# A two-block hybrid layer on one core: all four routing chunks of token tiles 1 to 3 placed beside the preceding tile's experts

## Chip, cores and metric

One core of a Trainium2 chip runs the whole program. The metric is device time in microseconds (us) from one launch, as a median over runs.

## What is computed

Everything is fp32, batch 1, 256 tokens, model width 1024. A first block (gated recurrent branch, delta-rule branch, feed-forward) is followed by two hybrid layers. Each hybrid layer mixes four kinds of attention and then applies a product-key expert layer, which is the part at issue:

```python
def block(xi):                                   # 128 tokens
    qv = (xi @ wq).reshape(B, 128, 8, 2, 128)    # 8 heads, two halves
    s = jnp.einsum('bthpc,hpnc->bthpn', qv, sub_keys)
    top_s, top_i = lax.top_k(s, 16)              # 16 best of 128 keys per half
    cand_s = top_s[..., 0, :, None] + top_s[..., 1, None, :]
    best_s, best_j = lax.top_k(cand_s..., 16)    # 16 best of 256 pairs
    expert = take(cand_i, best_j); gate = softmax(best_s)
    act = gelu(einsum('btd,bthkd->bthk', xi, u_tab[expert]))
    return einsum('bthk,bthkd->btd', gate * act, v_tab[expert])
```

So each token picks 8 x 16 = 128 of 16384 experts, and each expert is one row of 1024 numbers in `u_tab` and one in `v_tab`. In the kernel the two tables lie side by side in one tensor `puv` with rows of 2048 numbers (8 KB).

## The kernel before, in words

**Tiles.** The 256 tokens are two tiles of 128, and there are two hybrid layers, so the second half of the program works through four token tiles, numbered 0 to 3 (tiles 0 and 1 are layer 0, tiles 2 and 3 layer 1). Tile i+2 needs the result of tile i, and some state goes from tile i to tile i+1, but the mixing part of tile i+1 does not need the experts of tile i. The kernel therefore runs the mixing part of tile i+1 beside the experts of tile i.

**Experts.** Expert step n = 128 i + k serves the k-th chosen expert of all 128 tokens of tile i. `fetch` on POOL (L2274) gathers 128 rows of `puv` (1 MB) into one of six buffers `GR` (`PING` = 6), after expert n-6 has left its buffer. `expert_ve` on DVE (L2290) multiplies the u half by the tokens and sums. `expert_ac` on ACT (L2259, L2261, L2264) applies gelu and the gate and scales the v half. `expert_pe` on PE (L2246) adds the eight transposed 128x128 pieces into PSUM banks 6 and 7.

**Query and route.** Per tile these come in four chunks c of two heads. `query_pe` (L2121) multiplies by the weights `pwq` in 8 steps, two loads of 1 MB, and `query_ac` (L2132) copies the result out. `route_pe` (L2142) does the key scores, `route_ac` (L2153) copies them to `S1`, and `route_ve` takes the two rounds of top 16 on DVE in steps (first instruction L2164, last before the indices are ready L2223) and writes the indices `IX` and gates. A chunk is 8 query and 20 route steps. Chunk c gives the experts 32c to 32c+31 of its tile: `fetch` waits for `TV[i, c, "ix"]` at those numbers.

**The plan.** The list `plan` (from L259) sets one order for all engines: each engine plays the steps of the plan in this order, and those in which it has nothing to do cost it nothing. An engine executes in order, so an instruction that waits holds back everything behind it there. Beside the 128 experts of tile i there is a main lane, the end of tile i-1 (`fin`, 8 of its steps) and all of `tile_steps(i + 1)`, spread by `weight` over 118 experts; `tile_steps` gives `fm` and `tm` (projections), `gates`, `nsa` and `core` woven together (attention), `mix` (output projection and norm), and `query` and `route` of chunk 0. A second lane holds chunks 1 to 3 of tile i itself, spread over its own first 33 experts. Tile 0 has no preceding tile and its first part runs ahead of all experts.

**Loads.** SP issues the weight loads of the four tiles (`loads2`, L2496) into a ring of five slots of 1 MB (`RING2`), in the order of first use in the plan. A load is issued when the load five before it has been used up. Queries of a tile read eight `pwq` loads, and the other parts of a tile about forty loads. The scratch that tile 0's own query and route chunks use (`QP`, `S1` and so on, from `scr`) is also that of the next tile's attention, so these must not overlap in the plan.

Of the kernel before, what the change touches and what calls it, by code (L numbers as in the profile page):

```python
# [40 lines left out]
def weave(parts, filler=None):  # L41


    left = {name: steps for name, steps, _ in parts}
    owed = dict.fromkeys([name for name, _, _ in parts] + ([filler[0]] if filler else []), 0.0)
    order = []
    while any(left.values()):
        for name, _, rate in parts:
            if left[name]:
                owed[name] += rate  # L50
                while owed[name] >= 1 and left[name]:
                    owed[name] -= 1
                    left[name] -= 1
                    order.append(name)
        if filler:
            owed[filler[0]] += filler[1]
            while owed[filler[0]] >= 1:
                owed[filler[0]] -= 1
                order.append(filler[0])
    return order  # L60
# [18 lines left out]
def build(nc, A, out):  # L79
# [4 lines left out]
    with ctx:  # L84
# [159 lines left out]
        R2, R3, R4, R6, R8 = range(2), range(3), range(4), range(6), range(8)  # L244
# [12 lines left out]
        NE = 512  # L257
        weight = dict(fm=1.06, ht1=1.5, tm=1.7, gates=1.7, nsa=1.2, core=1.5, mix=1.5, query=1.06, route=0.7, fin=1.0)

        def tile_steps(i):  # L260
            front = ["fm"] * 28 + ["ht1"] * (i == 0) + ["tm"] * 4 + weave([("tm", 10, 1), ("core", 7, 0.7)])
            attend = weave([("gates", 32, 1), ("nsa", 23, 1), ("core", 14, 0.7)])
            return front + attend + ["mix"] * 24 + ["query"] * 8 + ["route"] * 20

        plan = [(s, 0) for s in tile_steps(0)[:-36]]
        plan += [(s, 0) for s in tile_steps(0)[-36:]]
        for i in RI:
            placed_at = [(128.0 * i + k, ("e", 128 * i + k)) for k in range(128)]
            placed_at += [(128.0 * i + 1.1 + 0.1 * k, ("fin", i - 1)) for k in range(4) if i >= 1]
            lane = [("fin", i - 1)] * 8 * (i >= 1) + [(s, i + 1) for s in (tile_steps(i + 1) if i < 3 else [])]  # L270
            total, done = sum(weight[s] for s, _ in lane), 0.0
            for s in lane:
                placed_at.append((128.0 * i + 1.5 + 118 * done / total if i < 3 else 128.0 * i + 1.5 + done, s))
                done += weight[s[0]]
            lane = []
            for c in R3:
                lane += [("query", i)] * 8 + [("route", i)] * 20
            for n, s in enumerate(lane):
                placed_at.append((128.0 * i + 0.2 + 33.0 * n / len(lane), s))
            plan += [s for _, s in sorted(placed_at, key=lambda x: x[0])]  # L280
        plan += [("e", NE), ("e", NE + 1)] + [("fin", 3)] * 12

# [5 lines left out]
                    nsa=[("cw", 0, 0, 2)], gates=[("g", n, 2 * n, 4 * (n // 2) + 3) for n in range(16)],  # L288
                    mix=[("b", n, 2 * n + 2, 2 * n + 3) for n in R4] + [("o", n, 12 + n, 12 + (n | 1)) for n in R4] + [("ga", 0, 19, 21)],
                    query=[("q", n, 4 * n, 8 * (n // 2) + 7) for n in R8], fin=[("gf", 0, 8, 9)])  # L290
        step, nth2, last2 = {}, {}, {}
        for at_, s in enumerate(plan):
            n = step[s] = step.get(s, -1) + 1
# [2351 lines left out]
```

## Time and profile before

| what | value |
|---|---|
| runs (device time) | 2823.6, 2828.5 and 2821.54 us, median 2823.6 |
| profiled execution, span from first to last instruction | 2818.2 us |
| PE busy in it | 2309.7 us (82%) |
| DVE busy | 1353.8 us (48%) |
| ACT busy | 1299.6 us (46%) |
| POOL busy | 742.4 us (26%) |
| DMA moved | 839.32 MB, mean 298 GB/s |
| first to last expert fetch | 1098.5 to 2790.9 us |

The profile covers one execution. Its page gives the span of instructions only, without a time of its own for what lies around it: the span is 5.4 us under the median of the three runs. Busy shares are over the whole span, in which two very different halves lie: up to 1098.5 us the first block and tile 0's mixing part, then the 512 experts.

### The profile page before, as it was taken

The page shows a single profiled execution, that of the slowest core. Times are in us where ns is not written, and L with a number is a line of the kernel's source. Part 1 is how long each engine was busy: PE and PEld are TensorE (multiplying, and loading weights), DVE is VectorE, ACT ScalarE, POOL GpSimd, SP SyncE. Part 2 cuts the span into 40 slices and gives each one's busy share as a digit, 9 for nine tenths or more (in the row PEclk, how much of TensorE's full clock was granted, in tenths as well). Part 3 has the DMA queues.
Part 4 walks back from the last instruction along what each step waited for, and adds up shares of the span by engine and source line. Part 5 has one row for each costly group of instructions (what it writes and reads, how often), then busy time and mean ns, then how long its engine had stood idle before and what let it go on. Part 6 is the DMA issues. An engine that isn't in the chain of part 4 may idle for free.

```text
span 2818.2 us, 33729 instructions
## 1 busy us (share of the span) xinstructions
PE 2309.7 (82%) x13336; PEld 1955.2 (69%) x13336; DVE 1353.8 (48%) x3183; ACT 1299.6 (46%) x2327; POOL 742.4 (26%) x614
## 2 busy tenths in 40 slices
PE   7989998999999995887876877787788787666666
PEld 6878887876875875776755866666777675565554
DVE  3552333321002234666456765545766545686444
ACT  2751113100000212577745576844658764566665
POOL 0021112200000001233333323333323333334554
PEclk9989999999999997999996999898799899776665
DMA  5321211133434666999999999999999999999997
GB/s 241 117 90 60 78 65 45 53 138 144 151 150 156 253 236 258 421 408 416 399 421 403 411 421 419 408 421 421 390 420 410 414 383 420 393 365 363 417 421 311
DMA packets 109998, 839.32 MB, mean 298 GB/s; under 512 B 12176, under 2 KB 12432, under 8 KB 13968
## 3 DMA queue, kind: packets, MB, share of 16 engines
q0 software_dynamic: 73728, 536.90, 46.6%
q1 hardware_dynamic: 36112, 300.25, 27.0%
q8 instruction: 106, 1.74, 0.2%
q14 instruction: 52, 0.43, 0.0%
HBM read 836.06 MB, written 1.05 MB: 297 GB/s over the span
## 4 chain that ended last, share of the span: by engine, by line
PE 48%; DMA 24%; DVE 12%; ACT 10%; issue 4%; POOL 2%; SPq 0%; POOLq 0%; DVEq 0%; ACTq 0%
DMA mem<-in_puv,mem 23%; PE psm L442 11%; PE psm L2246 6%; PE psm L450 5%; DVE mem L2290 4%; PE psm L755 4%; PE psm L1809 4%; ACT mem L2264 3%; PE psm L2121 3%; PE psm L1350 3%; PE psm L1453 2%; PE psm L2008 2%; ACT L2259 1%; PE psm L1501 1%; PE psm L446 1%
## 5 line engine op out<-in xcount | busy, mean ns | idle before, releaser
L2246 PE MATMUL psm<-mem 128*128 128x128 f32 x4096 | 682.1, 322 | 363.6 <-ACT mem L2264 361.2
L2274 POOL DMA_INDIRECT mem<-in_puv,mem x512 | 621.1, 1213 | 1059.9 <-PE psm L2246 993.3
L2246 PEld LDWEIGHTS psm<-mem 128*128 128x128 f32 x4096 | 566.5, 167 | 475.7 <-ACT mem L2264 459.8
L2290 DVE CUSTOM_DVE_ANT_0 mem<-mem 128x1024 f32<-128x1024 f32 x512 | 624.5, 1225 | 471.3 <-DMA mem<-in_puv,mem 470.8
L2264 ACT ACTIVATE mem<-mem 128x1024 f32<-128x1024 f32 x512 | 588.8, 1150 | 16.7
L442 PE MATMUL psm<-mem 128*128 128x256 f32 (+2 forms) x1376 | 313.0, 390 | 3.1 <-DVE mem L1290 1.5
L2259 ACT ACTIVATE mem<-mem 128x1 f32<-128x1 f32 x512 | 101.9, 199 | 437.7 <-DVE mem L2290 434.5
L442 PEld LDWEIGHTS psm<-mem 128*128 128x128 f32 x1376 | 261.8, 192 | 53.2 <-issue 14.8
L1809 PE MATMUL psm<-mem 128*128 128x256 f32 x1024 | 256.0, 398 | 0.5 <-ACT mem L1529 0.5
L450 PEld LDWEIGHTS psm<-mem 128*128 128x128 f32 x1440 | 187.2, 196 | 49.1 <-issue 21.4
L450 PE MATMUL psm<-mem 128*128 128x128 f32 x1440 | 199.3, 283 | 22.6 <-DVE mem L1125 6.8
L1809 PEld LDWEIGHTS psm<-mem 128*128 128x128 f32 x1024 | 197.3, 202 | 26.9 <-ACT mem L1529 0.9
L2261 ACT ACTIVATE mem<-mem 128x1 f32<-128x1 f32 x512 | 150.8, 295 | 16.6
L755 PE MATMUL psm<-mem 128*128 128x256 f32 x576 | 151.6, 387 | 0.0
L2121 PE MATMUL psm<-mem 128*128 128x128 f32 x1024 | 139.3, 293 | 2.3 <-DMA mem<-in_pwq 1.0
L2121 PEld LDWEIGHTS psm<-mem 128*128 128x128 f32 x1024 | 133.6, 210 | 4.5 <-DVE mem L2104 2.0
L1035 ACT ACTIVATE mem<-psm 128x512 f32<-128x512 f32 x64 | 38.2, 597 | 201.5 <-PE psm L450 134.6
L1453 PE MATMUL psm<-mem 128*128 128x128 f32 x896 | 113.5, 280 | 6.9 <-DVE mem L2334 3.8
L1453 PEld LDWEIGHTS psm<-mem 128*128 128x128 f32 x896 | 108.0, 197 | 8.2 <-DVE mem L2334 4.5
L755 PEld LDWEIGHTS psm<-mem 128*128 128x128 f32 x576 | 100.7, 195 | 7.9
L446 PE MATMUL psm<-mem 128*128 128x128 f32 (+1 forms) x352 | 60.6, 310 | 54.0 <-DVE mem L484 13.3
L446 PEld LDWEIGHTS psm<-mem 128*128 128x128 f32 (+1 forms) x352 | 45.8, 158 | 68.4 <-issue 26.2
(364 smaller groups left out, 2365.7 us busy)
## 6 DMA issues: line engine op xcount, KB each, us to landing
mem<-in_w2g SPq DMA_DIRECT2D x64, 1024.0 KB
mem<-in_w SPq DMA_DIRECT2D x18, 2048.0 KB, 8.2
mem<-in_pwq SPq DMA_DIRECT2D x32, 1024.0 KB
mem<-in_w2f SPq DMA_DIRECT2D x28, 1024.0 KB
mem<-in_wgu SPq DMA_DIRECT2D x11, 2048.0 KB, 7.7
mem<-in_w2t SPq DMA_DIRECT2D x20, 1024.0 KB
mem<-in_w2b SPq DMA_DIRECT2D x16, 1024.0 KB
mem<-in_w2o SPq DMA_DIRECT2D x16, 1024.0 KB
```

The lines of the kernel that those rows point to most:

```text
L442: m = pe.matmul(o, lhs(k), rhs(k), start=start and k == ks[0], stop=stop and k == ks[-1])
L446: return pe.transpose(o, i, ident[0:i.shape[0], 0:i.shape[0]])
L450: m = pe.matmul(b[:, u * 128:u * 128 + 128], lhs(u), rhs(u), start=True, stop=True)
L755: m = pe.matmul(o, W[:, k, c0:c0 + 128], HT[:, k, :], start=k == 0, stop=k == 7)
L1453: m = pe.matmul(o, W[:, k, h * 128:h * 128 + 128], HT[:, k, tsl(t)], start=k == 0, stop=k == 7)
L1809: m = pe.matmul(gates_bank(i, n // 2)[:, n % 2 * 256:n % 2 * 256 + 256], HT[:, k, tsl(t)], W[:, k, :], start=k == 0, stop=k == 7)
L2121: m = pe.matmul(o, W[:, k, h * 128:h * 128 + 128], HT[:, k, tsl(t)], start=k == 0, stop=k == 7)
L2246: m = pe.matmul(bank(6 + c // 4)[:, tsl(c % 4)], GR[n % PING][:, 1024 + c * 128:1152 + c * 128], ident, is_transpose=True, start=k == 0 an ...
L2261: ac.activation(co, co, ACT.Copy, scale=g).then_inc(oa.up(), 1)
L2264: ac.activation(v, v, ACT.Copy, scale=co).then_inc(EA.next(n), 1)
L2274: po.indirect_dma_start(GR[n % PING], None, A[f"puv{i // 2}"], bass.IndirectOffsetOnAxis(ap=IX[i % 2][:, k:k + 1], axis=0)).then_inc(gsem[ ...
L2290: ve.tensor_tensor_reduce(out=GR[n % PING][:, 0:1024], in0=GR[n % PING][:, 0:1024], in1=X[:, i % 2, :], scale=1.0, scalar=0.0, op0=MUL, op ...
```

## The change

`EARLY = (1, 2, 3)` names tiles whose four query and route chunks are all part of `tile_steps`, and so of the main lane beside the preceding tile's experts. The second lane is empty for these, and for tile 0 it holds chunks 1 to 3 over 28 experts in place of 33. For tile 1, 16 of the 32 `gates` steps go ahead of the woven attention, which keeps tile 1's attention behind tile 0's own chunks. No instruction is added or removed; line numbers of the changed kernel are 4 higher from the plan on.

```diff
--- before.py
+++ after.py
@@ -257,10 +257,13 @@
         NE = 512
         weight = dict(fm=1.06, ht1=1.5, tm=1.7, gates=1.7, nsa=1.2, core=1.5, mix=1.5, query=1.06, route=0.7, fin=1.0)
 
+        EARLY = (1, 2, 3)
+
         def tile_steps(i):
             front = ["fm"] * 28 + ["ht1"] * (i == 0) + ["tm"] * 4 + weave([("tm", 10, 1), ("core", 7, 0.7)])
-            attend = weave([("gates", 32, 1), ("nsa", 23, 1), ("core", 14, 0.7)])
-            return front + attend + ["mix"] * 24 + ["query"] * 8 + ["route"] * 20
+            ahead = 16 * (i in EARLY and i - 1 not in EARLY)
+            attend = ["gates"] * ahead + weave([("gates", 32 - ahead, 1), ("nsa", 23, 1), ("core", 14, 0.7)])
+            return front + attend + ["mix"] * 24 + (["query"] * 8 + ["route"] * 20) * (4 if i in EARLY else 1)
 
         plan = [(s, 0) for s in tile_steps(0)[:-36]]
         plan += [(s, 0) for s in tile_steps(0)[-36:]]
@@ -273,10 +276,11 @@
                 placed_at.append((128.0 * i + 1.5 + 118 * done / total if i < 3 else 128.0 * i + 1.5 + done, s))
                 done += weight[s[0]]
             lane = []
-            for c in R3:
-                lane += [("query", i)] * 8 + [("route", i)] * 20
+            lane = []
+            if i not in EARLY:
+                lane = ([("query", i)] * 8 + [("route", i)] * 20) * 3
             for n, s in enumerate(lane):
-                placed_at.append((128.0 * i + 0.2 + 33.0 * n / len(lane), s))
+                placed_at.append((128.0 * i + 0.2 + 28.0 * n / len(lane), s))
             plan += [s for _, s in sorted(placed_at, key=lambda x: x[0])]
         plan += [("e", NE), ("e", NE + 1)] + [("fin", 3)] * 12
```

Two places show what moves. PE, one whole chunk, from the key scores of one chunk (L2142, or L2146 in the changed kernel) to those of the next; L2121 (L2125) are query matmuls and L2246 (L2250) the eight transposes of each expert. Before, this is from tile 3's chunk 1 to its chunk 2, beside tile 3's own experts:

```order
L2142 MATMUL psm<-mem 128x128 x4
L2246 MATMUL psm<-mem 128x128 x64
L2121 MATMUL psm<-mem 128x128 x12
L2246 MATMUL psm<-mem 128x128 x8
L2121 MATMUL psm<-mem 128x128 x8
L2246 MATMUL psm<-mem 128x128 x8
L2121 MATMUL psm<-mem 128x128 x12
L2246 MATMUL psm<-mem 128x128 x8
L2142 MATMUL psm<-mem 128x128 x4
```

With the change, from tile 3's chunk 0 to its chunk 1, beside tile 2's experts:

```order
L2146 MATMUL psm<-mem 128x128 x4
L2250 MATMUL psm<-mem 128x128 x48
L2125 MATMUL psm<-mem 128x128 x12
L2250 MATMUL psm<-mem 128x128 x8
L2125 MATMUL psm<-mem 128x128 x8
L2250 MATMUL psm<-mem 128x128 x8
L2125 MATMUL psm<-mem 128x128 x12
L2250 MATMUL psm<-mem 128x128 x8
L2146 MATMUL psm<-mem 128x128 x4
```

Before, 64 transposes (8 experts) follow the key scores and 3 more lie among the query matmuls, 11 experts per chunk; now 6 and 3, 9 experts (in the order of the changed kernel a chunk in the main lane has 8 or 9, and over the nine distances between the four chunks of tiles 1 to 3 the mean is 8.8). The same 32 query matmuls and 4 score matmuls stand among fewer experts.

SP, the last loads of the program, from the output projection's weights of tile 3 (`in_w2b`, `in_w2o`; `in_rows` are norm weights). Before:

```order
L2496 DMA mem<-in_w2b 128x2048 x4
L2496 DMA mem<-in_w2o 128x2048 x4
L2496 DMA mem<-in_rows 128x2048
L2496 DMA mem<-in_pwq 128x2048 x4
L2496 DMA mem<-in_rows 128x2048
L2496 DMA mem<-in_pwq 128x2048 x4
L2496 DMA mem<-in_rows 128x2048
L2507 DMA out<-mem 128x1024 x2
```

and with the change:

```order
L2500 DMA mem<-in_w2b 128x2048 x4
L2500 DMA mem<-in_w2o 128x2048 x4
L2500 DMA mem<-in_rows 128x2048
L2500 DMA mem<-in_pwq 128x2048 x8
L2500 DMA mem<-in_rows 128x2048 x2
L2511 DMA out<-mem 128x1024 x2
```

The last `in_rows` before the output belongs to tile 3's final norm, the one before it to tile 2's. Six of tile 3's eight query loads stood around tile 2's norm weights, where tile 3's own experts run; now all eight are ahead of it.

## Rows read from the trace of the kernel before

**Rows 1.** the page, busy time and the 40 slices of 70.5 us
```profile
PE 2309.7 (82%) x13336; PEld 1955.2 (69%) x13336; DVE 1353.8 (48%) x3183; ACT 1299.6 (46%) x2327; POOL 742.4 (26%) x614
...
PEclk9989999999999997999996999898799899776665
DMA  5321211133434666999999999999999999999997
GB/s 241 117 90 60 78 65 45 53 138 144 151 150 156 253 236 258 421 408 416 399 421 403 411 421 419 408 421 421 390 420 410 414 383 420 393 365 363 417 421 311
```

**Rows 2.** stretches with busy time of each engine, the last tile without and with routing
```profile
core 0: us, PE busy (x) PEld busy (x) DVE busy (x) ACT busy (x) POOL busy (x), PEclk, DMA share, GB/s
2577.00:2777.00 200.00, 137.54 (x635) 110.08 (x634) 98.39 (x160) 130.17 (x238) 117.86 (x80) 0.64 1.01 420
2500.00:2580.00 80.00, 54.89 (x341) 48.48 (x340) 57.80 (x180) 50.51 (x90) 31.73 (x28) 0.72 0.89 328
```

**Rows 3.** waits from 1130 us on: who for whom, us in total, times, longest
```profile
POOL mem L2274 <- PE psm L2246: 976.2, 436, 8.1
DVE mem L2290 <- DMA mem<-in_puv,mem: 461.3, 294, 5.0
```

**Rows 4.** the same view, own chunks 1 to 3 of tiles 1 and 2
```profile
1560.00:1680.00 120.00, 98.06 (x752) 91.72 (x751) 86.10 (x275) 73.81 (x128) 36.38 (x33) 0.96 1.01 414
2015.00:2130.00 115.00, 98.16 (x718) 91.03 (x716) 83.72 (x269) 73.19 (x125) 34.89 (x31) 0.91 1.01 417
```

**Rows 5.** DVE in order of time, last two own chunks of tile 3: start, us, line
```profile
2508.14 0.88 DVE L2164 MAX8 mem<-mem 128x8 f32<-128x128 f32 x4 [7.00 <-ACT mem L2153]
...
2530.06 0.19 DVE L2223 SCALAR_TENSOR_TENSOR mem<-mem 128x32 uint32<-128x32 f32 x1
...
2543.06 0.68 DVE L2164 MAX8 mem<-mem 128x8 f32<-128x128 f32 x3 [7.22 <-ACT mem L2153]
...
2564.99 0.19 DVE L2223 SCALAR_TENSOR_TENSOR mem<-mem 128x32 uint32<-128x32 f32 x1
```

**Rows 6.** stretches, the last own chunk whole, then its two halves
```profile
2530.10:2565.10 35.00, 25.10 (x161) 22.23 (x160) 27.17 (x90) 21.55 (x38) 12.55 (x11) 0.74 0.89 330
2530.10:2543.10 13.00, 12.56 (x102) 12.32 (x102) 5.41 (x16) 8.92 (x17) 4.25 (x4) 0.90 0.81 307
2543.10:2565.10 22.00, 12.54 (x62) 9.91 (x60) 21.76 (x75) 12.63 (x22) 8.30 (x7) 0.65 0.94 344
```

**Rows 7.** by line: DVE over 2495 to 2565 us, PE over 2530.1 to 2565.1 us
```profile
L2290 DVE CUSTOM_DVE_ANT_0 mem<-mem 128x1024 f32<-128x1024 f32 x22 | 26.4, 1216 | 0.9 <-DMA mem<-in_puv,mem 0.9
...
L2246 PE MATMUL psm<-mem 128*128 128x128 f32 x89 | 16.7, 345 | 9.9 <-ACT mem L2264 9.9
L2121 PE MATMUL psm<-mem 128*128 128x128 f32 x64 | 8.8, 301 | 0.0
```

**Rows 8.** stretches, tile 3's chunk 0 and the 10 us behind it
```profile
2385.00:2431.00 46.00, 26.82 (x187) 23.23 (x185) 31.38 (x88) 22.96 (x41) 15.77 (x15) 0.83 1.01 421
2430.00:2440.00 10.00, 5.32 (x25) 5.29 (x26) 7.64 (x17) 8.28 (x17) 3.15 (x3) 0.50 0.75 288
```

**Rows 9.** DVE in order of time, chunk 0 of tile 3: first and last step
```profile
2407.84 0.88 DVE L2164 MAX8 mem<-mem 128x8 f32<-128x128 f32 x4
...
2431.04 0.19 DVE L2223 SCALAR_TENSOR_TENSOR mem<-mem 128x32 uint32<-128x32 f32 x1
```

**Rows 10.** stretches, gates and attention of tiles 1, 2 and 3
```profile
1231.00:1418.00 187.00, 150.38 (x968) 129.62 (x967) 103.73 (x225) 132.54 (x235) 71.49 (x59) 0.93 1.00 409
1679.00:1870.00 191.00, 148.95 (x917) 127.70 (x916) 97.83 (x224) 137.94 (x245) 67.20 (x59) 0.91 1.01 415
2125.00:2322.00 197.00, 160.52 (x1010) 139.13 (x1007) 105.69 (x229) 139.86 (x243) 70.30 (x62) 0.92 0.99 401
```

**Rows 11.** stretch of tile 1's second and third own chunk, first experts of tile 0
```profile
1141.00:1231.00 90.00, 72.68 (x497) 65.78 (x496) 59.06 (x190) 59.10 (x101) 23.28 (x22) 0.91 1.01 414
```

**Rows 12.** the page, DMA issues by source
```profile
mem<-in_pwq SPq DMA_DIRECT2D x32, 1024.0 KB
```

## The prediction

> **What bounds the kernel now.** I read the page first [rows 1]. PE is busy 82% of the span, which looks like the bound, but the DMA line says otherwise for the second half: from slice 17 on, where the expert fetches begin, it shows 9 in all but one slice, at 399 to 421 GB/s in most. The best view of what this means is the last tile, where only experts are left [rows 2]: 200 us at DMA share 1.01 and 420 GB/s, with PE, DVE and ACT at half to two thirds. The waits agree [rows 3]: DVE's expert step waited 461 us for the gathers. So in the second half the kernel moves a fixed number of bytes at up to 421 GB/s, and a stretch costs time only where the rate is lower. One load or one expert fetch is 1.049 MB, which is 2.49 us at 421 GB/s; I count in these.
>
> Where is the rate lower? Mainly in the last tile, between 2500 and 2580 us [rows 2]: 328 GB/s over 80 us, a loss of 80 x (1 - 328/421) = **17.7 us**. There tile 3's own chunks 2 and 3 stand beside its own experts and no other tile's work exists. The same kind of chunk beside tiles 1 and 2 [rows 4] runs at 414 and 417 GB/s, since `fm` and `tm` of the next tile bring loads of their own to fill the rate. So a routing chunk is harmless beside a stage with many loads, and costs time without one.
>
> **How long one chunk takes when loads don't cover it.** The two index writes (L2223) of tile 3's last chunks are at 2530.1 and 2565.0 us [rows 5], 35 us apart with 11 experts between. In these 35 us DVE is busy 27.2 us [rows 6]: 11 experts at 1.22 us plus the read-out, some 1.30 us each, so 14.3, and 12.9 us for the chunk's top-16 work. It falls into two halves. In the first, 13 us, DVE mostly waits, 7.2 us in one piece, for the copy of the scores (L2153) [rows 5], while PE is busy 12.6 of 13 us with query matmuls and backed-up transposes [rows 6]. In the second, 22 us, DVE is busy 21.8. The queries alone are 8.8 us of PE per chunk [rows 7]. PE cannot start the next chunk's queries early: in its order they stand behind transposes of experts that DVE has not reached. So PE's half and DVE's half follow one another, whatever DMA could do.
>
> **The change, part by part.**
>
> *Tile 3's own chunks go.* Its experts then run like the 200 us of [rows 2] from the end of tile 2's norm on. Gain: the 17.7 us. The fewer query loads there (six of 1 MB) are no gain, they move to the stage before. **-17.7 us.**
>
> *Four chunks in a row beside the preceding tile's experts.* Chunk 0 stands there already: 46 us at 421 GB/s, then 10 us at 288 [rows 8]. It is covered by what is in flight, up to six fetches and the ring's five loads, and the drop behind it shows that the cover is then used up. I take chunk 0 as unchanged. Behind it now come three more per tile, nine in all, and what is beside them is only 8.8 experts and two query loads each [rows 12]: 10.8 MB, or 26.9 us of transfer. How long does each take? From the 35.0 us, 2.2 experts of 1.30 us fewer on DVE, 32.1 us, if the 7.9 us in which DVE idles stay. Low bound: part of the idle goes as well, as fewer transposes lie before the queries (2.2 experts at PE's 16.7/11 = 1.5 us [rows 7], 3.3 us): 28.8. High bound: chunk 0's DVE half took 23.2 us with only six experts [rows 9]; with the 13 us of the other half, 36.2. The nearest row is the tail's own cycle, so I stay by 32.1 and add half a microsecond because chunk 0's DVE half was the longer one: 32.6 us. Loss per chunk 32.6 - 26.9 = 5.7, nine times: **+51 us** (bounds 9 x 1.9 = 17 and 9 x 9.3 = 84). SP's queue is no extra wait here: the query loads follow each other in the ring as before. The cover is not renewed between chunks, as a ring slot frees only with the queries and a buffer only with its expert.
>
> A page states a higher ceiling: the Trainium skill, "Perfetto Trace Analysis", section Roofline, takes about 120% of 358 GB/s, thus 430, as what a single core can reach. By that figure as an estimate the transfers of a chunk would be 26.4 us and the loss nearly 5 us larger over nine chunks; the trace holds 420 to 421 [rows 2, 8] and I stay with it.
>
> *The own lane of tiles 1 and 2 is empty.* That stage was at 414 and 417 GB/s [rows 4], bound by bytes, and stays so with fewer. Gain at most 120 x (1 - 414/421) = 2 us; the wait of `fin` stays. **0.** If DMA did not cover it, 0 would be wrong, but it is what ends last there.
>
> *The other stages get fewer experts.* The main lane now holds more, over the same 118 experts, so gates and attention have about 41 experts where 57 ran in the 187 to 197 us of [rows 10]. Bytes per step fall, PE's work per step doesn't. Before: PE busy 149 of 191 us in tile 2's stretch. Less 16 experts at 1.2 us (1.5 at granted clock 0.74 [rows 6, 7], here 0.91), 130; the transfers are 41 + 17 loads, 144 us. So PE goes from 78% to 90%, still under the bytes, yet with less room. The three stretches already lose 5, 3 and 9 us against 421 GB/s. Between no more loss and twice this, 0 to +17, I take **+8**.
>
> *Tile 0's own chunks in 28 experts for 33, tile 1's gates ahead.* Before, 414 GB/s with PE busy 73 of 90 us [rows 11]. 16 gates steps cost PE and DMA about the same as the mix there; bounds 0 and +5, taken as 0, with bytes from tile 1's `fm`, `tm` and gates as the cover.
>
> Sum: -17.7 + 51 + 8 = **+41 us**. The profiled span of 2818.2 would become 2859; its distance of 5.4 us to the median lies in what surrounds the span and in scatter, so on the median of 2823.6 I forecast **2865 us**. Bounds: -17.7 + 17 = -1 and -17.7 + 84 + 17 + 5 = +88.
>
> **Rivals.**
>
> *A, faster: the bytes cover the chunks.* If the four chunks together with what is in flight never let the rate fall below 421, only the 17.7 us of tile 3 are left: 2806 us. The place is chunks 1 to 3 beside the preceding tile; it decides at 26.9 + 17.7/9 = 28.9 us per chunk, under which the whole is a gain. The Trainium skill, "Perfetto Trace Analysis", section Identifying the Most-Contended Engine, says to go by the engine with the highest occupancy; by that, DMA is the one here and moving DVE's work within a stage that DMA bounds is free. For it: chunk 0 ran at 421 GB/s [rows 8], and the own lanes too [rows 4]. Against it: the tail's 35 us cycles with PE and DVE taking turns [rows 6], and the 10 us at 288 right after a single chunk. 10%.
>
> *B, no change: cover for about half.* The chunks overlap better than in the tail, 29 to 30 us each, and tile 3's gain pays. Sum within 8.5 us of zero: 2824 us. For it: the granted clock is 0.65 in the DVE half and 0.90 in the other [rows 6], and where it stays up PE's half is shorter. Against: the same alternation. 8%.
>
> *C, slower still: PE becomes the bound of gates and attention.* If PE's idle there is dependency and not slack, the 16 experts fewer save little time, 10 us per tile instead of 3: three times 10, plus 51 less 17.7, gives 2887 us or more. For it: in the stretch of tile 3 PE was busy 160.5 of 197 us and the rate only 401 [rows 10]. 10%.
>
> That the change does not do what it says is not open: the order of both engines shows it.
>
> **How the numbers follow.** A measurement of this kernel tells a difference of about 0.3%, 8.5 us, from none. The forecast (cycle 31 to 35 us, 2835 to 2885 us) has 72%, A 10%, B 8%, C 10%. The forecast and C are slower by over 0.3%, 0.82; B is the same, 0.08; A is faster, 0.10. For 8 in 10 the range leaves out A, part of B and part of C: 2828 to 2895 us.
>
> **What would show it.** In the changed profile: three times per expert tile, a stretch of some 100 us before the next tile begins with 340 to 360 GB/s, each chunk 31 to 35 us from one index write to the next, DVE's wait for the score copy some 7 us each time, and the DMA line of the page at 8 there; the last tile at 420 GB/s from its first experts on, its fetches over in about 325 to 330 us. Index writes 27 us apart and 421 GB/s throughout would prove me wrong and A right; gates and attention under 390 GB/s would be C.

## The result, and the profile after

The changed kernel takes 2923.2 us (median of 4 runs, 2919.9 to 2929.7), the kernel before 2822.6 us in the same comparison: ratio 1.0365, 95% interval 1.0343 to 1.0387. I had forecast a loss of 41 us, 2865 us with a range of 2828 to 2895; it is 100 us. The direction was right, the size lies outside the range.

The page of the changed kernel, busy time and the 40 slices (now of 73 us), against [rows 1]:

```profile
PE 2351.5 (81%) x13336; PEld 1992.3 (68%) x13336; DVE 1354.7 (46%) x3183; ACT 1304.8 (45%) x2331; POOL 748.5 (26%) x614
...
PEclk9989999999999998898977888987699998766666
DMA  6221111234435569899998999998899999799997
GB/s 245 106 95 71 62 51 44 80 130 149 168 136 225 219 228 374 355 402 376 369 365 328 389 404 417 405 421 331 346 404 385 379 412 394 294 358 421 421 421 322
```

PE, DVE and ACT are busy for the same time within 2%; the same work is done. One thing was said wrongly ahead of the result: instructions are added, four on ACT (x2331 against x2327), all of them `ACT_TABLE_LOAD` of 1.28 us, 5.1 us together. They are not what makes the difference, as e2 and e10 below have 2327 and still lose 45 and 54 us. The DMA line, 9 nearly throughout before, now dips to 8 or 7 in every tile but the last, and the rates fall to 294 and 328 GB/s in places. The four chunks of tiles 1, 2 and 3, without their chunk 0, and a stretch of the last tile (columns as in [rows 2]):

```profile
1487.00:1592.00 105.00, 65.15 (x426) 59.30 (x425) 75.74 (x252) 54.78 (x96) 30.48 (x28) 0.78 0.88 341
1969.00:2071.00 102.00, 62.59 (x419) 57.15 (x418) 75.01 (x251) 53.01 (x94) 31.24 (x27) 0.75 0.88 343
2455.00:2558.00 103.00, 64.46 (x418) 58.95 (x417) 74.09 (x249) 52.99 (x93) 30.86 (x26) 0.75 0.81 303
2600.00:2800.00 200.00, 138.35 (x635) 110.81 (x636) 98.71 (x160) 130.88 (x238) 121.48 (x80) 0.64 1.01 421
```

The first three are the regions that I had described: 341, 343 and 303 GB/s with DVE busy for about three quarters of them. The last tile runs as foretold, 421 GB/s. DVE in order of time in the last region shows the cycles and the waits, against [rows 5] (L2227 is the index write, L2168 the first top-16 step):

```profile
2455.07 0.18 DVE L2227 SCALAR_TENSOR_TENSOR mem<-mem 128x32 uint32<-128x32 f32 x1
...
2487.93 0.18 DVE L2227 SCALAR_TENSOR_TENSOR mem<-mem 128x32 uint32<-128x32 f32 x1
...
2502.36 0.49 DVE L2168 MAX8 mem<-mem 128x8 f32<-128x128 f32 x2 [8.33 <-ACT mem L2157]
...
2521.37 0.19 DVE L2227 SCALAR_TENSOR_TENSOR mem<-mem 128x32 uint32<-128x32 f32 x1
...
2539.37 0.49 DVE L2168 MAX8 mem<-mem 128x8 f32<-128x128 f32 x2 [11.46 <-ACT mem L2157]
...
2558.35 0.19 DVE L2227 SCALAR_TENSOR_TENSOR mem<-mem 128x32 uint32<-128x32 f32 x1
```

Index writes are 32.9, 33.4 and 37.0 us apart here, over all nine chunks 31.9 to 37.0, mean 34.3. Where four experts stand between an index write and the next scores, DVE's wait for these is 7.0 to 8.3 us and the cycle 32.8 us in the mean (four cycles); where five do, the wait is 9.3 to 11.5 us but for one of 6.3, and the cycle 35.6 us (five cycles).

**Where the 100 us went.** I cut both traces at DVE's marks (index writes, first step of the mix, norm, first step of the final part `fin`) and took for each piece its length times (1 - rate/421), as in the prediction. The sums are worked out from the stretches view, from 1100 us to tile 3's final norm, and are in us of lost transfer:

| stage | before | after | difference |
|---|---|---|---|
| tile 0's own chunks 1 to 3 | 2.8 | 13.3 | +10.5 |
| projections, attention and mix of tile 1 | 5.3 | 20.9 | +15.6 |
| the same of tile 2, with what own lane there is beside it | 4.6 | 11.8 | +7.2 |
| the same of tile 3 | 11.9 | 21.1 | +9.2 |
| chunk 0 of tiles 1 to 3 | 0.0 | 0.0 | 0 |
| the nine chunks that were moved, beside the preceding tile | none | 67.4 | +67.4 |
| from the last chunk to `fin`, three times | 9.0 | 19.5 | +10.5 |
| last tile from `fin` on | 28.0 | 8.2 | -19.8 |
| sum | 61.6 | 162.2 | +100.6 |

The spans differ by 100.0 us. That the two agree proves nothing by itself: both kernels move the same 839.32 MB, so whatever time is lost must show as a lower rate somewhere. The table says which stages lose it, not why. Two thirds are the nine chunks; the 20 us won in the last tile are there as well; and 43 us are in stages for which I had set 8.

The stages ahead of the routing in the changed kernel: end of tile 0's own lane, attention of tile 1, and the whole of tile 2's and tile 3's projections and attention, against [rows 10, 11]:

```profile
1178.00:1233.00 55.00, 37.59 (x207) 33.17 (x208) 31.47 (x106) 35.62 (x58) 9.32 (x9) 0.81 0.87 338
1233.00:1400.00 167.00, 140.79 (x823) 121.63 (x822) 83.13 (x187) 111.39 (x189) 48.50 (x44) 0.87 0.93 376
1618.00:1875.00 257.00, 210.21 (x1344) 184.35 (x1344) 120.62 (x267) 169.95 (x301) 78.29 (x74) 0.89 0.99 402
2097.00:2360.00 263.00, 216.95 (x1424) 192.31 (x1425) 129.65 (x273) 173.25 (x303) 80.76 (x73) 0.92 0.96 387
```

PE is busy 68%, 84%, 82% and 82% of these: below the 90% that I had feared for attention, and yet bytes are lost, which a bound by an engine's busy time does not explain.

### The profile page after: what moved, and what is told of

Its sections match the earlier page's. It is cut to its first block, busy times and chain, and to the rows that moved or that the text cites. A ratio compares the mean times of both kernels' runs of the same rounds, so it can differ in the third digit from the quotient of the medians.

```text
span 2918.2 us, 33733 instructions
## 1 busy us (share of the span) xinstructions
PE 2351.5 (81%) x13336; PEld 1992.3 (68%) x13336; DVE 1354.7 (46%) x3183; ACT 1304.8 (45%) x2331; POOL 748.5 (26%) x614
## 2 busy tenths in 40 slices
DMA packets 109998, 839.32 MB, mean 288 GB/s; under 512 B 12176, under 2 KB 12432, under 8 KB 13968
## 4 chain that ended last, share of the span: by engine, by line
PE 52%; DMA 17%; DVE 14%; ACT 10%; issue 4%; POOL 2%; SPq 0%; POOLq 0%; DVEq 0%; ACTq 0%
DMA mem<-in_puv,mem 16%; PE psm L446 11%; PE psm L2250 7%; PE psm L454 5%; PE psm L1813 5%; DVE mem L2294 4%; PE psm L759 4%; PE psm L1457 3%; ACT mem L2268 3%; PE psm L2125 3%; PE psm L1354 3%; PE psm L2012 2%; PE psm L1505 2%; ACT L2263 2%; PE psm L450 1%
## 5 line engine op out<-in xcount | busy, mean ns | idle before, releaser
L2250 PE MATMUL psm<-mem 128*128 128x128 f32 x4096 | 703.5, 329 | 416.1 <-ACT mem L2268 413.3
L2250 PEld LDWEIGHTS psm<-mem 128*128 128x128 f32 x4096 | 583.8, 171 | 529.5 <-ACT mem L2268 509.4
L446 PEld LDWEIGHTS psm<-mem 128*128 128x128 f32 x1376 | 262.7, 193 | 52.8 <-issue 14.8
L454 PEld LDWEIGHTS psm<-mem 128*128 128x128 f32 x1440 | 187.5, 196 | 49.1 <-issue 21.5
L454 PE MATMUL psm<-mem 128*128 128x128 f32 x1440 | 199.6, 284 | 22.7 <-DVE mem L1129 6.8
L1813 PEld LDWEIGHTS psm<-mem 128*128 128x128 f32 x1024 | 194.6, 198 | 26.6 <-issue 1.2
L2125 PE MATMUL psm<-mem 128*128 128x128 f32 x1024 | 145.8, 303 | 4.4 <-DVE mem L2108 3.2
L2125 PEld LDWEIGHTS psm<-mem 128*128 128x128 f32 x1024 | 140.9, 220 | 6.0 <-DVE mem L2108 4.7
L1457 PE MATMUL psm<-mem 128*128 128x128 f32 x896 | 109.3, 278 | 0.7 <-ACT mem L1372 0.7
L759 PEld LDWEIGHTS psm<-mem 128*128 128x128 f32 x576 | 101.1, 196 | 8.0
L1457 PEld LDWEIGHTS psm<-mem 128*128 128x128 f32 x896 | 105.6, 195 | 0.9 <-DVE mem L1377 0.9
## 6 DMA issues: line engine op xcount, KB each, us to landing
mem<-in_w2t SPq DMA_DIRECT2D x20, 1024.0 KB, 11.9
```

Source lines behind the costliest of these rows:

```text
L446: m = pe.matmul(o, lhs(k), rhs(k), start=start and k == ks[0], stop=stop and k == ks[-1])
L454: m = pe.matmul(b[:, u * 128:u * 128 + 128], lhs(u), rhs(u), start=True, stop=True)
L759: m = pe.matmul(o, W[:, k, c0:c0 + 128], HT[:, k, :], start=k == 0, stop=k == 7)
L1457: m = pe.matmul(o, W[:, k, h * 128:h * 128 + 128], HT[:, k, tsl(t)], start=k == 0, stop=k == 7)
L1813: m = pe.matmul(gates_bank(i, n // 2)[:, n % 2 * 256:n % 2 * 256 + 256], HT[:, k, tsl(t)], W[:, k, :], start=k == 0, stop=k == 7)
L2125: m = pe.matmul(o, W[:, k, h * 128:h * 128 + 128], HT[:, k, tsl(t)], start=k == 0, stop=k == 7)
```

## The experiments

In most runs theory A is the prediction's mechanism: a chunk's query half on PE and its route half on DVE follow one another, and 8.8 experts and two loads don't fill that time. Theory B, in its forms, puts the loss elsewhere. All ratios are to the kernel before, run beside it; the changed kernel stands at 1.0365.

**e1: queries of the next chunk among this chunk's route steps.**

```diff
+        def chunks_(n):
+            out = ["query"] * 8
+            for _ in range(n - 1):
+                out += (["route"] * 2 + ["query"]) * 8 + ["route"] * 4
+            return out + ["route"] * 20
-            return front + attend + ["mix"] * 24 + (["query"] * 8 + ["route"] * 20) * (4 if i in EARLY else 1)
+            return front + attend + ["mix"] * 24 + chunks_(4 if i in EARLY else 1)
```

> The changed kernel with the eight query steps of chunk c+1 played among the first sixteen route steps of chunk c for tiles 1 to 3, and nothing else. Theory A (the loss is PE's query half and DVE's route half of a chunk following one another): the halves overlap, the index writes come closer to 27 or 28 us apart instead of 34, and of the 75 us that the rate loses in these regions some 50 come back: 2860 to 2880 us. Theory B (the loss comes from the other stages having fewer experts beside them, and the regions only show it): 2915 to 2930 us, no change.

2865.3 us, ratio 1.0158 (1.0131 to 1.0184): 58 us came back, as theory A said. The same three regions in its trace:

```profile
1494.00:1572.00 78.00, 48.08 (x336) 44.44 (x336) 71.69 (x244) 49.92 (x86) 27.81 (x24) 0.83 1.01 421
1957.00:2035.00 78.00, 46.40 (x320) 41.81 (x320) 69.88 (x241) 48.23 (x83) 27.27 (x23) 0.86 1.01 414
2427.00:2504.00 77.00, 47.70 (x330) 42.58 (x328) 69.67 (x240) 48.23 (x83) 25.56 (x24) 0.82 0.95 375
```

421, 414 and 375 GB/s where it was 341, 343 and 303, in 78 us where it was 102 to 105. DVE is busy about 90% of it. Its wait for the scores, from DVE's order of time:

```profile
2458.18 0.49 DVE L2174 MAX8 mem<-mem 128x8 f32<-128x128 f32 x2 [1.75 <-ACT mem L2163]
...
2485.24 0.29 DVE L2174 MAX8 mem<-mem 128x8 f32<-128x128 f32 x1 [1.75 <-ACT mem L2163]
```

is 1.75 us here, and 0.9 to 1.9 in the eight chunks that wait, in place of 6 to 11. Lost in the nine chunks: 10 us, from 67. The same steps and loads stand there in another order, beside 70 experts where it was 79, and yet less is lost: the alternation is shown to be the cause of this part. The attention stages lose about what they lost (15.6, 13.5 and 22.3 us, where it was 18.3, 11.8 and 21.0).

**e2: only tile 3 early** (`EARLY = (3,)`; all own lanes 28 experts, tile 3's gates ahead).

> EARLY = (3,): only tile 3's four chunks stand beside tile 2's experts; tiles 1 and 2 keep their own lane, as short as tile 0's in the changed kernel, 28 experts, and tile 3 has the 16 gates steps ahead. Theory A: one region of three extra chunks, 25 to 32 us lost, 20 us gained in the last tile, little else: 2825 to 2840 us. Theory B: the single dense lane costs 10 to 20 us more than that and the gates steps ahead 10 more: 2845 to 2860 us.

2867.7 us, ratio 1.0175 (1.0141 to 1.0208), above what either theory gave. It mixes several edits; e3 to e5 take them apart in part.

**e3: own lanes shortened from 33 to 28 experts in the kernel before.**

```diff
-                placed_at.append((128.0 * i + 0.2 + 33.0 * n / len(lane), s))
+                placed_at.append((128.0 * i + 0.2 + 28.0 * n / len(lane), s))
```

> The kernel before with 28.0 for 33.0 in the own lane of every tile and nothing else. Theory A: these chunks have cover by the next tile's loads, so no change, 2820 to 2828 us. Theory B: the start of each tile gets too dense for PE and in-order waits, 4 us and more per tile: 2835 us and more.

2858.0 us, ratio 1.0138 (1.0108 to 1.0168): 35 us for five experts' room, theory B's side and far more than I thought. In tile 3, which has no loads to cover them, the three chunks run at

```profile
2480.00:2586.00 106.00, 67.11 (x416) 59.98 (x414) 78.87 (x251) 52.46 (x92) 29.91 (x28) 0.73 0.83 304
```

304 GB/s with 29.6 us lost in the three pieces between index writes, 17 before. The rest is spread over the stages ahead of the routing, 6 to 8 us more in each of the three tiles. Only the spacing of the routing steps was changed: the closer they stand, the fewer bytes are beside them.

**e4: 16 of tile 1's gates steps ahead of its attention, in the kernel before.**

```diff
-            attend = weave([("gates", 32, 1), ("nsa", 23, 1), ("core", 14, 0.7)])
+            ahead = 16 * (i == 1)
+            attend = ["gates"] * ahead + weave([("gates", 32 - ahead, 1), ("nsa", 23, 1), ("core", 14, 0.7)])
```

> The kernel before with 16 of tile 1's 32 gates steps ahead of its woven attention, and nothing else. Theory A: no change within 5 us, since bytes bind. Theory B: the attention that is left has fewer loads and matmuls beside it and ends in a stretch with no load at all, 10 to 17 us as between 1370 and 1400 us of the changed kernel's trace: 2833 to 2840 us.

2836.7 us (seven runs, 2826.7 to 2840.7), ratio 1.0041 (1.0023 to 1.0060), some 12 us slower, 7 to 17 by the interval: theory B. The stretches view shows it at the end of tile 1's attention, where the gates steps and their loads have run out:

```profile
1410.00:1450.00 40.00, 30.26 (x150) 25.74 (x150) 22.86 (x49) 28.91 (x51) 9.78 (x10) 0.67 0.72 263
1239.00:1447.00 208.00, 162.39 (x970) 141.11 (x970) 104.11 (x226) 135.17 (x236) 69.66 (x59) 0.86 0.95 384
```

263 GB/s for 40 us, in which no load is issued; the whole attention stage loses 18.3 us where it lost 5.3 (the trace is of the slowest of the seven runs, so rather the high end). This is a part of the change that I had set at nothing.

**e5: one region, nothing else that can be avoided** (the changed kernel with `EARLY = (3,)`, `ahead = 0`, own lanes `33.0 if i < 2 else 28.0`), and **e6: the same with e1's weaving.**

> EARLY = (3,), no gates steps ahead, own lanes of tiles 0 and 1 over 33 experts as before and tile 2's over 28: one region of three extra chunks, with as little else changed as the scratch allows. Theory A (the region itself loses): 25 to 32 us lost in it, 20 us won in the last tile, 5 us for the denser lane beside it: 2833 to 2842 us. Theory B (what e2 lost is in the short own lanes and the gates, the region is free): 2803 to 2815 us.

> The kernel of e5 with the query steps of chunk c+1 among the route steps of chunk c in that region. Theory A: of the 25 to 32 us of the region about 20 come back, so 2815 to 2824 us, about 20 us under e5. Theory B: like e5.

2842.0 us, ratio 1.0075 (1.0049 to 1.0100), and 2824.0 us, ratio 1.0012 (0.9994 to 1.0031). The region of three chunks, e5 and then e6:

```profile
2377.00:2480.00 103.00, 64.14 (x419) 58.64 (x417) 74.14 (x249) 52.99 (x93) 30.53 (x27) 0.75 0.81 307
```

```profile
2387.00:2465.00 78.00, 48.20 (x321) 43.12 (x320) 70.19 (x242) 48.30 (x83) 27.20 (x23) 0.82 0.95 376
```

27.9 us lost in e5's and 8.3 in e6's, and the runs differ by 18. Both came out as theory A said, e5 at the upper end of its range, e6 at the top of its own: one tile moved costs 20 us, weaving gives nearly all of it back, and then the move is worth nothing. The stage of tile 3 ahead of the region loses 19 us in e5 and 29 in e2, which has 16 of tile 3's gates steps ahead of its attention: e4's effect at another tile.

**e7: only tile 3's own chunks woven, in the kernel before.**

```diff
+            if i < 3:
+                lane = ([("query", i)] * 8 + [("route", i)] * 20) * 3
+            else:
+                lane = [(s, i) for s in chunks_(3)]
```

> The kernel before, with only tile 3's own chunks 1 to 3 woven (queries of the next chunk among the route steps of this one), all else the same. Theory A: the alternation is what holds the rate at 328 GB/s from 2500 to 2580 us, so 10 to 15 us of the 17.7 are won: 2807 to 2813 us. Theory B (DVE's own work is the bound there, or the wait for the gathers): no change, 2820 to 2825 us.

2810.9 us, ratio 0.9966 (0.9950 to 0.9983), within theory A's range and, by the medians, 11 us faster than the kernel before. The 328 GB/s of [rows 2] became

```profile
2500.00:2560.00 60.00, 38.09 (x240) 33.13 (x240) 53.71 (x178) 42.09 (x73) 23.07 (x20) 0.77 1.00 392
```

**e8: the changed kernel with tile 0's own lane over 33 experts again** (`28.0` to `33.0`).

> The changed kernel with tile 0's own lane over 33 experts again in place of 28. If the short lane costs here what it costs in e3 at the start of tile 0 (some 8 us between 1190 and 1240 us): 2912 to 2917 us. If it is nothing without the other lanes: 2920 to 2926 us.

2928.4 us, ratio 1.0392 (1.0357 to 1.0426): above both expectations, and its interval overlaps that of the changed kernel (1.0343 to 1.0387), so slower is not shown; its fastest run, 2927.5 us, is 10 us above what a gain by the longer lane would have given. With the gates steps ahead, tile 0's last chunk then stands among more of tile 1's steps: the third chunk lost 17.0 us there, 10.8 in the changed kernel, and the attention behind it 15.1, where it was 18.3. The short lane is no loss in this place.

**e9: tile 1's remaining gates steps spread over its whole attention** (rate 0.7 in the weave).

> The changed kernel with tile 1's 16 remaining gates steps spread over its whole attention (rate 0.7 in the weave, where it was 1), so that loads and matmuls do not end seven iterations before the attention does. Theory A (the 17 us lost between 1370 and 1410 us come from a stretch with dependent small steps and no loads): 10 us come back, 2910 to 2916 us. Theory B (the attention is slow there whatever stands beside it): 2920 to 2926 us.

2922.1 us, ratio 1.0361 (1.0344 to 1.0378), no change, as theory B said. Tile 1's attention and mix lost 14.7 us in place of 20.9, but its chunks lost 2.9 us more and the stage of tile 2 behind them 3.1. So that loads run out is not the whole of what e4 showed.

**e10: tiles 2 and 3 early, without gates ahead** (own lanes of 33 experts for tile 0 and 28 for tile 1).

> EARLY = (2, 3) without gates steps ahead, tile 0's own lane over 33 experts and tile 1's over 28. Two regions of three extra chunks. If regions add up as in e5 (one region and its denser stages +40, last tile -20): 2821 + 80 - 20 = 2875 to 2885 us, and tile 1's region with the gates steps ahead is then the remaining 40 to 45 us of the change. If a second region is cheaper, as the stages between are bound by bytes: 2855 to 2870 us.

2873.0 us, ratio 1.0199 (1.0182 to 1.0216), 54 us over its kernel before. By its time it lies between the two ranges, by the difference at the low end of the first (54 to 64 over 2821). So the cost grows 20 us (one tile), 54 (two), 100 (three): the first has the last tile's 20 us on its side, the second is a bare region with its denser stage, and the third brings one more region together with tile 1's gates ahead and tile 0's lane, 46 us.

**e11: tile 3's own chunks over 72 experts in place of 33, in the kernel before.**

```diff
-                placed_at.append((128.0 * i + 0.2 + 33.0 * n / len(lane), s))
+                placed_at.append((128.0 * i + 0.2 + (33.0 if i < 3 else 72.0) * n / len(lane), s))
```

> The kernel before with tile 3's own chunks spread over 72 of its experts in place of 33, 24 experts to a chunk, in no other order. Theory A (a chunk costs only where the bytes beside it are fewer than its two halves take, here 24 experts or 60 us of transfer against some 52 us): nearly all of the 17.7 us are won, 2803 to 2809 us, and more than in e7. Theory B (each alternation drains the gathers whatever the distance): 2815 to 2825 us.

2805.2 us, ratio 0.9954 (0.9937 to 0.9970), as theory A said. Tile 3's routing stage now reads

```profile
2460.00:2640.00 180.00, 123.90 (x757) 107.56 (x757) 127.44 (x333) 118.33 (x214) 88.52 (x69) 0.74 1.01 413
```

with 3.3 us lost in three chunks, which are 60 to 62 us apart. The alternation is still there, the steps are in the same order; it costs nearly nothing once 24 experts stand beside each chunk. This is the fastest kernel of the study by its median (its interval overlaps e7's), 14 us under the kernel before, and it changes one number.

**e12: e1 and e9 together.**

> The changed kernel with both, queries of chunk c+1 among the route steps of chunk c as in e1, and tile 1's remaining gates steps spread as in e9. If the two losses are separate: e1 less what e9 won, 2853 to 2860 us; if they hide one another: 2862 to 2868 us.

2858.8 us, ratio 1.0144 (1.0127 to 1.0161), against 1.0158 for e1: within the first range, but the difference to e1 lies inside both intervals. It settles nothing on the gates.

**e13: e1 with smaller planner weights for query and route**, so that the stages ahead get more of the experts.

```diff
-        weight = dict(..., query=1.06, route=0.7, fin=1.0)
+        weight = dict(..., query=0.8, route=0.4, fin=1.0)
```

> The kernel of e1 (woven) with smaller weights for query (0.8 for 1.06) and route (0.4 for 0.7) in the planner, so that the four chunks take about 6.3 experts each in place of 8.8 and projections, attention and mix of the next tile get the others. Nothing else moves. Theory A (the stages ahead of the routing lose because too few experts stand between their dependent steps): in e1 these stages lost 13 to 22 us per tile; now 7 to 13, some 20 us less over the tiles, while the woven chunks get shorter than their DVE work allows for their bytes (21 us of DVE against 8.3 loads, 20.7 us) and lose 5 to 15: total 2850 to 2862 us. Theory B (these stages lose whatever the number of experts beside them): they lose 13 to 22 us as before and the total is 2868 us or more.

2883.2 us, ratio 1.0221 (1.0197 to 1.0245), on theory B's side. One place did what theory A said, the end of tile 0's own lane, then tile 1's attention:

```profile
1176.00:1217.00 41.00, 31.64 (x203) 27.71 (x202) 29.77 (x100) 32.62 (x52) 9.14 (x9) 0.94 1.01 414
1217.00:1414.00 197.00, 160.74 (x925) 138.41 (x924) 95.88 (x212) 126.88 (x218) 58.43 (x53) 0.85 0.93 377
```

Where e1 (and the changed kernel, 338 GB/s) lost 10 us, 0.8 are lost. But the attention stages lose 20.6, 10.1 and 22.9 us, e1's 15.6, 13.5 and 22.3, so about the same, while the nine chunks went from 10 to 26 us and the stretches to `fin` from 19 to 26. More experts beside these stages (51 for 42 in tile 1's attention, 78 for 69 and 77 for 70 in the stages of tiles 2 and 3) did not help them. So more room won something in the routing, but not in attention.

## Why the prediction was right in direction and wrong in size

**The bound** was read rightly: the last tile and each tile's chunk 0 still run at 421 GB/s, and what the change costs stands in stretches below that. (A chunk's "10.8 MB" of the prediction are 10.8 transfers, 11.3 MB; their 26.9 us are right.) **Tile 3's gain** of 17.7 us is measured at 19.8. **The covered chunk 0** lost nothing before and nothing after. **Rival A** (the bytes cover the chunks, 28.9 us each or less) is refuted by the trace: no cycle is under 31.9 us. In e1, with the alternation taken out, the cycles are 27 to 28 us and the bytes do cover them. **Rival B**, no change, is out with it. **Rival C** (PE becomes the bound of gates and attention, 2887 us or more) is the one case that holds the measured time, and its 10 us per tile is what these stages lost more, 32 us in all. Its sign, under 390 GB/s, showed in tile 1's attention (376) and tile 3's stage (387), not in tile 2's (402). Its mechanism is not shown: PE is busy 82 to 84% there.

**"How long does each take?", 32.6 us, was too short.** Mean 34.3, so 1.7 us times nine, 15 us: lost 67 instead of 51. What failed is the assumption that DVE's 7.9 us of idle stay when experts go: over the three regions they are 9.0 to 9.8 us per chunk. With four experts in that half it nearly held (32.8 us); where the rounding of the plan puts five there, the wait grows, to 11.5 us at most. PE's half begins with PE waiting for ACT, and ends with ACT waiting for PE. PE, ACT and POOL in order of time around the index write at 2521.4:

```profile
2525.00 1.97 PE L2250 MATMUL psm<-mem 128*128 128x128 f32 x8 [4.69 <-ACT mem L2268]
2526.77 4.54 PE L2125 MATMUL psm<-mem 128*128 128x128 f32 x24
...
2532.01 1.95 PE L2125 MATMUL psm<-mem 128*128 128x128 f32 x16
```

```profile
2521.70 0.23 ACT L2161 ACTIVATE mem<-mem 128x32 f32<-128x32 f32 x1 [3.71 <-DVE mem L2228]
2521.94 1.28 ACT L2263 ACT_TABLE_LOAD   x1
...
2523.80 1.15 ACT L2268 ACTIVATE mem<-mem 128x1024 f32<-128x1024 f32 x1
...
2536.66 0.60 ACT L2136 ACTIVATE mem<-psm 128x512 f32<-128x512 f32 x1 [6.91 <-PE psm L2125]
```

```profile
2518.99 1.25 POOL L2278 DMA_INDIRECT mem<-in_puv,mem  x1 [3.23 <-PE psm L2250]
2527.25 1.47 POOL L2278 DMA_INDIRECT mem<-in_puv,mem  x1 [7.01 <-PE psm L2250]
```

The chain crosses three engines. ACT has the exponential of the gates (L2161) in its order and waits 3.7 us for DVE's last routing step; only then come a table load and the next expert's scaling; PE waits 4.7 us for this; and POOL waits 7.0 us for PE's transposes, so that no gather is issued for 8 us. At the other end the copy of the queries (L2136) waits 6.9 us for PE. It stands ahead of an expert that DVE has finished, but PE reached that expert's transposes only behind its query and score matmuls and then waited just 0.4 us, so this second wait costs the gathers little. I had read the wait of DVE and not who stands in ACT's order.

**The stretch to `fin`** was not in the sum: 3 us each before, 6.5 after. Nearly all of it is lost in its first 10 us (173 GB/s behind tile 1's last chunk, 315 before, then 424), as the gathers in flight are used up by the chunk ahead of it; e13, with shorter chunks, made it 9. The region is longer than its chunks.

**"The other stages get fewer experts: +8" is the step that failed most**: measured +32, and with tile 0's own lane, which I had set at 0, +42.5. Of these, e4 shows some 12 for the gates steps ahead, which I had priced only as PE work against bytes and dismissed. I compared totals, PE's busy time with the transfers of a stage (90% expected, 82 to 84% measured), where the stage has single dependent steps that stand still for 4 to 10 us. e3 shows the same for the own lanes: 35 us for packing the same steps into 28 experts. What is shown is that packing costs.

What is left open is the cause within attention of tiles 2 and 3, 16 us. The loss is much the same in every kernel with all three tiles moved (for tile 3's attention 21.0, 22.3, 22.4 and 22.9 us in the changed kernel, e1, e9 and e13, against 9.3 before with 2.3 beside the own lane), so it is no scatter. e13 gave these stages 10% more experts and won nothing. An empty own lane is not needed for it: in e5 and e6 tile 2's own lane is there, over 28 experts, and tile 3's stage still loses 19 us; in e3, where no chunk is moved at all, it loses 18. The traces name one step that stands still for longer, DVE waiting for an exponential of ACT in `core`, here for tile 2, from `fin` to the mix, before and after (us in total, times, longest):

```profile
DVE mem L1698 <- ACT mem L1630: 4.7, 2, 2.7
```

```profile
DVE mem L1702 <- ACT mem L1634: 19.8, 4, 6.9
```

For tile 3 it is 7.7 and 20.5 us. In tile 2's stage eight kernels have this wait at 16 to 21 us and lose 10 to 15 us; six have it under 6 us and lose 4 to 5. But e10 loses 8 us there with 2.1 us of it, and e5 loses 19 us in tile 3's stage with 3.8 us of it, so it is not the whole cause, and no run changes it alone.

**The range** failed for the same reason: the high bound took each term's worst row, +17 and +5 for the stages, and no row of the kernel before shows a dense main lane without loads. The bound for an unseen arrangement came from an arrangement that was not like it. The high end of the sum, +88, would still have been short. Term by term, the sum of 41 us was 2 us too low in gain (-19.8 for -17.7), 16 short for the nine chunks, 10.5 for the stretches to `fin`, 24 for the other stages and 10.5 for tile 0's lane.

## What to carry to other kernels

In a kernel that moves bytes all the time, work that is "hidden" costs as soon as the bytes standing beside it take less time than its own dependent halves: count both per step of the plan, for a chain of equal chunks and not for one, and look in every engine's order for what waits there for another. Moving four such chunks to the same place loses on each; spreading them (24 experts to a chunk, e11) or weaving one chunk's PE half into the other's DVE half (e1, e7) wins, and e11 wins without a new order. The Trainium skill, "Perfetto Trace Analysis", section Optimization Strategy, says that a kernel with several regimes may gain from interleaving them; e11 agrees, 2805.2 us, and the change is the opposite case, a regime drawn together, at 2923.2 us. A plan by weights should also be tested for rounding: one expert more in a chunk's PE half went with a cycle 3 us longer.

## What was not expected of the hardware

PE's granted clock fell around these waits. In the fence of PE above, eight transposes of an expert took 1.97 us right after PE had waited 4.69 us, and 1.04 us when they were next to query matmuls a few us on; 24 query matmuls took 4.54 us, 189 ns each, and then 16 took 1.95 us, 122 ns each. The granted clock of these pieces, then of DVE's half behind them:

```profile
2525.00:2526.77 1.77, 1.77 (x9) 1.77 (x10) 1.77 (x5) 1.67 (x5) 0.00 (x0) 0.50 0.00 0
2526.77:2531.31 4.54, 4.54 (x27) 4.54 (x27) 1.14 (x2) 2.88 (x5) 1.47 (x1) 0.61 0.41 114
2531.31:2536.60 5.29, 5.29 (x50) 5.29 (x49) 0.00 (x0) 0.00 (x0) 1.89 (x2) 1.00 0.69 249
2539.40:2558.30 18.90, 7.60 (x38) 5.93 (x36) 18.59 (x68) 7.69 (x13) 6.78 (x5) 0.62 0.84 296
```

The first transposes ran at 0.50, which is the level of 1.2 GHz, the query matmuls behind them at 0.61, a mix, and the rest, with PE busy without a break since 2525.0, at 1.00, 2.4 GHz. The low part of PE's half is on the path, as DVE waits for its end. By these durations I estimate that about 2.5 us of the 11.5 us wait are due to the clock (0.9 for the transposes and 24 x 67 ns for the matmuls), a cost that rows of the kernel before had only as averages.
